# Two transformer blocks on one core: the RMS factor applied where results leave PSUM, squares folded in turn by VectorE, differential-output squares summed by ScalarE

## The reference, cut to what matters

```
xn = rms_norm(x, attn_norm[l])                      # x * rsqrt(mean(x*x)+eps) * gain
h  = xn @ w_in[l]                                   # [512, 2848], split in nine parts
c_q, c_kv = rms_norm(h_cq), rms_norm(h_ckv)         # "latent" parts, normed again
...
o_b = (softmax(q1 k1) - lam * softmax(q2 k2)) @ v   # 4 differential heads, each normed again
...
x = x + concat(o_a, o_b, o_c) @ w_o[l]
xn = rms_norm(x, ffn_norm[l])
g, u = split(xn @ w_gate_up[l])
x = x + (silu(g) * u) @ w_down[l]
```

## Time and profile before

| | us |
|---|---|
| median of 3 runs (3102.61 to 3106.01) | 3104.69 |
| the profiled execution | 3114.65 |
| its span | 3112.9 |
| its mean granted TensorE clock | 0.953 |

### The profile page before, as it was taken

The page is one execution under the profiler, slowest core; times in us unless marked ns, Lnnn a source line. Parts: engine busy times, 40 slices in busy tenths (PEclk is TensorE's granted clock), DMA queues, the critical chain, the costliest instruction groups (busy, mean ns, idle before and its releaser), DMA issues.

```text
span 3112.9 us, 33268 instructions
## 1 busy us (share of the span) xinstructions
PE 2881.9 (93%) x13076; PEld 2060.8 (66%) x13076; DVE 1189.6 (38%) x1632; ACT 949.3 (30%) x1558; POOL 810.6 (26%) x630
## 2 busy tenths in 40 slices
PE   5988989999899899899998999799998999899997
PEld 4965747888697575688885555445665444378886
DVE  2378614333318772443322233425323100243322
ACT  4448512222243862222221333323222100122222
POOL 5566502336637552133571000000000000000000
PEclk7999999999999999999998999898998999899998
DMA  4330013444422100334452110111112122133231
GB/s 101 86 86 17 1 39 104 142 138 145 137 75 70 39 1 22 104 115 142 137 161 87 41 41 27 28 27 41 41 41 54 54 64 71 41 95 95 86 93 65
DMA packets 382091, 230.25 MB, mean 74 GB/s; under 512 B 9228, under 2 KB 376716, under 8 KB 381936
## 3 DMA queue, kind: packets, MB, share of 16 engines
q1 hardware_dynamic: 379184, 223.04, 24.4%
q0 software_dynamic: 2224, 2.99, 0.8%
q10 hardware_dynamic: 528, 2.10, 0.2%
HBM read 226.01 MB, written 2.10 MB: 73 GB/s over the span
## 4 chain that ended last, share of the span: by engine, by line
PE 72%; DVE 13%; ACT 7%; DMA 6%; issue 2%; POOL 1%; SPq 0%; ACTq 0%; DVEq 0%; POOLq 0%
PE ps L728 61%; PE scores L728 8%; DMA raws<-in_w_down 4%; DVE R L1816 1%; PE ps L871 1%; ACT wH L1567 1%; DVE R L1926 1%; DVE R L520 1%; DVE R L521 1%; DVE R L511 1%; DVE R L512 1%; DVE R L515 1%; DVE xL L1922 0%; DVE x_lows L1922 0%; DVE wL L1948 0%
## 5 line engine op out<-in xcount | busy, mean ns | idle before, releaser
L728 PE MATMUL ps<-xH,wH 128*128 128x512 f32 x992 | 393.1, 396 | 12.0 <-DVE xL L1922 12.0
L728 PE MATMUL ps<-xH,wL 128*128 128x512 f32 x992 | 387.8, 391 | 0.0
L728 PE MATMUL ps<-xL,wH 128*128 128x512 f32 x992 | 387.7, 391 | 0.0
L638 POOL TENSOR_TENSOR U<-U 128x512 f32<-128x512 f32 x42 | 57.7, 1374 | 1193.2 <-ACT U L1390 1191.8
L1567 ACT ACTIVATE wH<-raws 128x2048 fp32r<-128x2048 f32 (+1 forms) x114 | 192.9, 1692 | 568.1 <-PE ps L728 393.6
L1948 DVE TENSOR_TENSOR wL<-raws,wH 128x2048 fp32r<-128x2048 f32 (+1 forms) x114 | 241.8, 2121 | 269.6 <-ACT wH L1567 262.7
L728 PE MATMUL ps<-R,ring 128*128 128x512 f32 x704 | 305.6, 593 | 2.9 <-DVE R L2166 1.6
L728 PE MATMUL ps<-U,ring 128*128 128x512 f32 (+4 forms) x640 | 270.5, 575 | 8.2 <-ACT R L1628 8.2
L728 PE MATMUL ps<-R 128*64 128x128 f32 (+3 forms) x1688 | 239.8, 332 | 37.5 <-DVE R L1835 10.2
L728 PEld LDWEIGHTS ps<-R 128*64 128x64 f32 (+2 forms) x1688 | 157.5, 165 | 135.1 <-issue 75.5
L728 PEld LDWEIGHTS ps<-R,ring 128*128 128x128 f32 x704 | 133.4, 190 | 170.7 <-issue 166.8
(11 more groups left out here) (344 smaller groups left out, 4275.5 us busy)
## 6 DMA issues: line engine op xcount, KB each, us to landing
raws<-in_w_gate_up SPq DMA_DIRECT2D x88, 512.0 KB, 5.2
ring<-in_w_in SPq DMA_DIRECT2D x34, 1024.0 KB, 6.4
spare<-in_w_ada SPq DMA_DIRECT2D x64, 512.0 KB, 4.0
raws<-in_w_down SPq DMA_DIRECT2D x32, 704.0 KB, 5.6
raws<-in_w_ffn_in SPq DMA_DIRECT2D x44, 512.0 KB, 4.7
ring<-in_w_in SPq DMA_DIRECT2D x32, 512.0 KB, 6.0
raws<-in_w_ffn_out SPq DMA_DIRECT2D x16, 704.0 KB, 4.3
ring<-in_w_o SPq DMA_DIRECT2D x5, 896.0 KB, 5.0
```

The costliest lines, as they stand in the source:

```text
L638: pg.do(nc.gpsimd.tensor_tensor(xn[:, 0, :], xn[:, 0, :], xn[:, k, :], ALU.add), folded if k == KT - 2 else None)
L728: return nc.tensor.matmul(o, a, b, start=first, stop=last)
```

## The change

1. **Factor after the product.** In the layers, VectorE writes x·gain only (`gained`), and ScalarE and VectorE split that. The factor goes in when results leave PSUM: by ScalarE's copy with a scale for the token-major pieces of W_IN (`scaled_out`), and in the FFN by VectorE, once on the gate before Silu and once on the product (`scaled_products`). The latent parts are left without it, since they are normed again; to be exact, eps over the squared factor is added to their sum of squares by one more product each (`square_sum`, operand `eps_`).
2. **Squares in turn.** ScalarE squares tile k as soon as it is there (`square_in_turn`), VectorE adds it up (`fold`) in place of GpSimd. TensorE takes the sums after the first gate group of an FFN (`stream_sums`), or after the first token group of layer 1. In layer 0 ScalarE squares the input in its own layout, four tiles of 128x1024, with the accumulator.
3. **Start.** The input comes in two halves behind the identity matrix, and the first W_IN piece's low part is VectorE's.
4. **Weights earlier.** The last W_O piece has a buffer of its own (`wo_last`), so that FFN weights are loaded and split before W_O ends; the first W_IN piece of layer 1 is loaded and split before the FFN of layer 0 ends. W_O is four pieces in both layers.
5. **Rotation.** It starts after the 16 differential sums, with a reciprocal of its own, and two of its steps go behind each of the 12 grouped-query sums.
6. **Differential-output squares.** ScalarE takes them with its accumulator, two of 128x128 in each of rounds 20 to 27; VectorE's four are gone.
7. **Tables.** A dummy Sqrt (`root_table`) sets ScalarE's table ahead of the root, at the start, at the W_O and FFN ends and before the second block's FFN. There GpSimd takes the low part of the first weight tile (`first_low`).

The diff, cut to its core:

```diff
-            return x_lows[:, k, :] if k < KT - 1 else x_low_last[:, :]
+            return UP[:, 2 * k:2 * k + 2, 0:256] if k < KT // 2 else xL1[:, k - KT // 2, :]
...
+        wo_last = R[:, 6656:6656 + 10 * 256].rearrange("p (k c) -> p k c", k=10)
...
+        DB_RING = [D_BANKS[1], D_BANKS[0]]
+        NB = SP[1][:, 0, :]
...
-        WO = [[(0, 384), (384, 768), (768, 1024)], [(0, 256), (256, 512), (512, 768), (768, 1024)]]
+        WO = [(0, 256), (256, 512), (512, 768), (768, 1024)]
...
-        OUTPUT_SQUARES_AT, OUTPUT_ROOT_AT = (21, 22, 23, 24), 26
+        OUTPUT_SQUARES_FROM, OUTPUT_ROOT_AT = 20, 27
...
+            def first_low(l):
+
+                g = l * NF
+                pool.wait_ge(wh_ready, g + 1)
+                pg.do(nc.gpsimd.tensor_tensor(wL[:, g % 2, :], raws[:, g % 2, :], wH[:, g % 2, :].bitcast(F32), ALU.subtract),
+                      first_wl_ready)
...
-                    q = a - l * N_ADA + ADA_FIRST
-                    if q >= FT + 4 and (q - FT) % 2 == 0:
-                        fold((q - FT) // 2 - 2)
-                fold(KT - 2)
-                pg.seen[sq_ready] += 1
+                if l + 1 < L:
+                    low_part(l + 1, 0)
...
+            def two_sums(bank, total, last):
+
+                for n, square in enumerate((total, last)):
                     if n == 0:
-                        pp.more(folded)
+                        pp.more(folded, KT - 2)
...
+            def stream_sums(l):
+
+                if l > 0:
+                    pe.wait_ge(inv_copied, l)
+                two_sums(NB, PTb[:, 0, :], PTb[:, 1, :]).then_inc(sums_full, 1)
...
-            def square_sum(k0, k1, src, ready):
+            def square_sum(k0, k1, src, ready, eps_):
                 bank = ab.fill(pe)
+                pp.more(lat_eps_ready)
+                mm(bank[:, :], ones[:, :], eps_, True, False)
                 for k in range(k0, k1):
                     pp.more(ready)
-                    ins = mm(bank[:, :], ones[:, :], src(k), k == k0, k == k1 - 1)
+                    ins = mm(bank[:, :], ones[:, :], src(k), False, k == k1 - 1)
...
+                            if l > 0 and a == c1 and t == 0:
+                                stream_sums(l)
...
-                folded_sums()
-                spread_roots(S)
+                if l < L:
+                    pe.wait_ge(a_free, ab.n)
+                else:
+                    folded_sums(X(0), X(KT - 1))
+                    spread_roots(S)
...
+                            if l < L and q == 0:
+                                if n == 0:
+                                    stream_sums(l)
+                                else:
+                                    pp.more(diag_ready)
+                                    mm(NB[:, :], ones[:, :], dg[:, :], True, True).then_inc(spread_full, 1)
...
-            sp.dma_start(xin, A["x"][0].rearrange("(t p) c -> p t c", p=P)).then_inc(x_in, 16)
-            sp.dma_start(ident[:, :], A["c_ident"][:, :]).then_inc(x_in, 16)
...
+            sp.dma_start(ident[:, :], A["c_ident"][:, :]).then_inc(x_in[0], 16)
+            for a in range(2):
+                half = slice(a * D // 2, (a + 1) * D // 2)
+                sp.dma_start(xin[:, :, half], A["x"][0].rearrange("(t p) c -> p t c", p=P)[:, :, half]).then_inc(x_in[a], 16)
...
-                for piece in layer_pieces(l):
-                    load(piece)
+                for j, piece in enumerate(layer_pieces(l)):
+                    if l > 0 and j == 0:
+                        sp.wait_ge(wl_ready, l * NF - 1)
+                    if l > 0 and j == 1:
+                        sp.wait_ge(*f_by[l * NF - 1])
+                    load(j, piece)
+                sp.wait_ge(ot_full, (l + 1) * (N_PAIR - N_DIFF) // TT)
+                for dst, src in wo_piece(l, *WO[-1])(None):
+                    sp.dma_start(dst, src).then_inc(wo_in, 16)
...
+            def square_in_turn(k):
+                ap.more(x_ready)
+                if k >= 2:
+                    act.wait_ge(folded, turns * (KT - 2) + k - 1)
+                ap.do(f(PTb[:, min(k, 1), :], xT[:, k, :], ACT.Square), sq_ready)
+
+            def root_table():
+                ap.do(f(unused[:, :], eps[:, :], ACT.Sqrt))
+
...
+            for t in range(TT):
+                ap.do(f(xin[:, t, :], xin[:, t, :], ACT.Square, accum_out=ssg[:, t:t + 1]))
+            ap.do(f(rt[:, :], ssg[:, :], ACT.Sqrt, bias=eps[:, :], scale=1.0 / D), root_ready)
...
+            def scaled_out(dst, src, t, sem=None):
+                ap.do(f(dst, src, ACT.Copy, scale=rt[:, t:t + 1]), sem)
...
+                    if 0 <= p_ - OUTPUT_SQUARES_FROM < 2 * TT:
+                        for n in range(2):
+                            t, h = divmod(2 * (p_ - OUTPUT_SQUARES_FROM) + n, BH)
+                            ap.do(f(vtmp[:, 0, 0:BV], O[:, t, h * BV:(h + 1) * BV], ACT.Square, accum_out=ssO[:, t, h:h + 1]))
...
+                root_table()
+                for k in range(KT):
+                    high_tile(xH[:, k, :], k)
+                    square_in_turn(k)
+                    if k >= 5 and k < 7:
+                        split_high(l, k - 5)
+                stream_root()
+                turns += 1
...
+                        if l < L:
+                            act.wait_ge(gate_scaled, n)
+                            ap.do(f(Pb[:, q % 2, :], Pb[:, q % 2, :], ACT.Silu), silu_ready)
...
-                def output_squares(t):
-                    if t == 0:
-                        dve.wait_ge(v_done, (l + 1) * N_DIFF)
-                    o = O[:, t, :]
-                    vp.do(v.tensor_tensor(vtmp[:, 0, 0:512], o, o, ALU.mult))
-                    vp.do(v.tensor_reduce(ssO[:, t, :], vtmp[:, 0, 0:512].rearrange("p (h d) -> p h d", h=BH), AX.X, ALU.add))
...
+                turning = chain(*[rotation(vp, v, t, T, rs, vtmp, 16, BD, gB, ropeB, bT_ready, l, 8, False) for t in range(TT)])
                 for c in range(GK):
                     for t in range(TT):
                         sums(ssG[:, t, c:GH:GK], (3, GD))
+                        next(turning)
+                        next(turning)
...
+                    gained(m, first_gain(l, KT))
+                    low_part_of(xH[:, m, :], xl(m), m)
+                    if m == 6:
+                        split_low(l, 0)
+                    fold(m)
+                split_low(l, 1)
+                vp.more(root_ready)
+                vp.do(v.reciprocal(rt[:, :], rt[:, :]))
+                vp.do(v.tensor_tensor(dg[:, :].rearrange("p (a b) -> p a b", a=TT), bc(ident[:, :], TT, 1),
+                                      bc(rt[:, :], P, 2), ALU.mult), diag_ready)
+                dve.wait_ge(spread_full, l + 1)
+                vp.do(v.tensor_copy(inv, NB[:, :]), inv_copied)
...
+            def gained(k, gain):
+                vp.do(v.tensor_scalar(Pb[:, k % 2, :], xT[:, k, :], gain(k), None, ALU.mult), scaled)
+
+            def fold(k):
+                nonlocal squares
+                squares += 1
+                if 1 <= k < KT - 1:
+                    dve.wait_ge(sq_ready, squares)
...
+            def scaled_products(l):
+                for j in range(FT):
+                    n = l * FT + j + 1
+                    dve.wait_ge(gate_full, n)
+                    vp.do(v.tensor_tensor(Pb[:, j % 2, :], A_BANKS[j % 2][:, :], inv, ALU.mult), gate_scaled)
+                    bank = db.take(dve)
+                    vp.more(silu_ready)
+                    t = PTb[:, 1, :]
+                    vp.do(v.tensor_tensor(t, Pb[:, j % 2, :], bank[:, :], ALU.mult), d_free)
+                    vp.also(silu_used)
+                    split_low(l, j + 2)
+                    vp.do(v.tensor_tensor(t, t, inv, ALU.mult))
+                    split(hH[:, j, :], hL[:, j, :], t, h_ready)
```

381 lines of the change are left out of this document (243 added, 138 removed).

## The result

| | before | with the change |
|---|---|---|
| median, us | 3104.72 (4 runs) | 3034.01 (4 runs, 3030.29 to 3040.21) |
| profiled execution, us | 3114.65 | 3035.83 |
| its span | 3112.9 | 3034.0 |
| its mean granted clock | 0.953 | 0.970 |

The ratio is 0.9775, with a 95% interval of 0.9757 to 0.9793: 70.7 us less by the medians. 94.3 less was forecast. The kernel is faster, as forecast, but by a quarter less: 3034.01 for 3010.4, a hundredth of a microsecond above the upper end of the range (3034). One run of the kernel before, among those taken beside the experiments, took 8896.47 us; it is left out of the ratios, and its cause is not known.

What follows compares the result with a forecast made beforehand. TensorE was taken as the bound, fully busy inside FFN tiles, with only its idle time between them to save. The terms summed to 94.3 us less, from a median of 3104.69 to 3010.4; range 2998 to 3034.

Steps and rivals of the forecast that it cites:

- Bound: FFN tiles: TensorE busy 238.00 of 238.00 us at full clock; only its idle time between such stretches can go.
- Entries: From W_O through tile 0 of both layers' FFNs: 13.6 us in place of 28.65, 29.8 saved for the two.
- The start: Program start: first W_IN piece done at 39.5 us, where it ended at 62.83; 23 saved, bounds 18 to 25.
- layer 1's second token group: Entry of layer 1: from last residual addition to this group's copy 8.3 us, for 26.8; 18.5 saved.
- The step that failed: W_O and down tiles: the fold's eight VectorE additions of 0.69 us lie beside them, with no cost counted.
- Rotation: Both layers: TensorE's 12.3 us of waiting go, plus 3 for the lower clock behind; 15.5 saved, bounds 12.3 to 16.6.
- Added: TensorE: four more products of the eps diagonals cost 4.0 us.
- Attention: Attention rounds: VectorE's squares moved to ScalarE save 3.7 us a layer, 7.4 in all, bounds -3 to 11.
- Second FFN: Second block's FFN entry: split leaves VectorE and table load comes ahead, 2.8 us saved; 0.9 if GpSimd blocks VectorE.
- VectorE in the FFN: 44 gate/up tiles: VectorE's two more operations of 0.69 us a tile cost 0, covered by its idle time.
- Rival B: W_IN pieces: GpSimd's low part blocks VectorE, TensorE waits at most 15 us in two layers; 3025, chance 0.15.
- Rival E: FFN gate path: Silu and VectorE's in-order list lengthen the 44 gate/up tiles, making the kernel slower; 3115, chance 0.03.

Runs made afterwards that it cites:

- run 10: The changed kernel with the loads of each layer's FFN weights held until W_O has ended: 3062.96 us, ratio 0.9845.
- run 1: The changed kernel with SyncE issuing the next FFN weight tile's load ahead of the conditioning load: 3013.93 us, ratio 0.9701.
- run 8: The changed kernel with the rotation steps behind all grouped-query sums again, its own early reciprocal kept: 3038.03 us, ratio 0.9760.
- run 7: The changed kernel with two more unused VectorE products of 128x512 in each of the 44 gate/up tiles: 3039.93 us, ratio 0.9777.
- run 5: The changed kernel with the second block's weight pieces starting at ring slot 2: 3034.44 us, ratio 0.9770; with its first FFN low part on VectorE too, 3031.87, 0.9755.
- run 6: The changed kernel with GpSimd's 22 small head-gain loads issued before its first low part, not between its low parts: 3045.94 us, ratio 0.9805.

## Why the forecast fell short

- **Bound.** Right for the gate/up tiles, which stayed at full rate, as in the earlier trace rows; wrong for the down tiles, for which no row was read.
- **Entries.** Right in mechanism. The FFN's gave 15.7 each for 14.9 (by the prediction's own 28.65 - 13.6 it is 15.05 each, 30.1 for the two and not 29.8); 11 of it hang on the weights and 4 to 5 on the rest (run 10). The start gave 24.4 at the end of the first piece for 23, less some 5 for the new stall; layer 1's second token group came 9.2 us behind the addition for 8.3.
- **The step that failed:** the term that puts everything laid beside the down tiles at nothing ("the fold's eight additions of 0.69 lie beside W_O and the down tiles", and ScalarE's new x tiles there with no word at all). Cover was read as idle time of the engine, and ScalarE was indeed idle, 6.7 us ahead of a high part. But its list is part of a loop through SyncE, whose turn was 8.1 us against tiles of 7.72 and which lived on a lead of 8 us. The turn became 8.98 in layer 0, by the x tiles (0.30) and the later landing of the loads (0.60), and 8.54 in layer 1, by the landing alone, and the lead was used up at down tile 4. That was 22.9 us; with one load moved in SyncE's list the same work costs nothing (run 1). VectorE's additions are not in the loop. No row said that the landing would be longer, and why it is stays open.
- **The rest of the sum.** With the 22.9 it would have been 71.4, against 70.7 by the medians. That this is so near is partly luck: single terms missed by up to 4 us, and both ways.
- **Rotation.** The wait went, as the term said (12.3 and the clock), but not for the reason given: without the interleaving only 0.83 us of waiting is left in each layer (run 8). Its size is right by luck.
- **Added.** The four eps products took 0.86 each, 3.4 for 4.0.
- **Attention.** 5.4 for 7.4 (1.4 and 4.0). The squares' rounds gain what was read, and a part is given back around the root.
- **Second FFN.** A loss of 0.3 to 1.2 for a gain of 2.8. The lock was priced (0.9), the slot of the ring was not looked at; with the slot right 1.1 to 1.2 are gained, near the table load alone.
- **VectorE in the FFN.** Zero, right (run 7). Rival B did not show: no wait on a W_IN low part stands in TensorE's list beyond the first piece. Rival E's mechanism was in the wrong place: the gate/up tiles had room, the down tiles had none.

## What to carry to other kernels

Idle time of an engine is cover only if the engine is not a link in a loop through other queues. Take one turn of each such loop (issue, landing, each operation behind it in its list, the wait that lets the next issue go), compare it with the tile, and look at how the lead changes from tile to tile: a lead that shrinks says that the loop is slower than it looks. And where a counter of buffers is started anew, see which piece comes to lie in the slot that somebody waits for.

## What the runs showed of the hardware

- A VectorE operation of 0.49 took 4.68 us beside a GpSimd operation of 4.50 and ended 0.3 behind it (after the change, 2633.72); one with a PSUM operand beside such a GpSimd operation kept its 0.75 (run 5, 2630.66).
- With 22 loads of 32 to 64 KB around them, the ring's pieces of 1 MB took twice as long to land: 12.0 us with them and 5.1 without for the fourth piece, 27.4 and 13.9 for the first three (run 6 and the change).
- The same 1344 products of the second block and what lies between them took 1022.2 to 1023.3 us in eleven executions (mean granted clock 0.961 to 0.963) and 1031.8 to 1032.0 in three (0.951), whatever the edit. Two profiled executions have to be aligned product by product before their difference is read.
- The FFN weights' loads landed later in every kernel with the change (second block's down weights: 4.6 or 4.7 us for 4.3 and 4.4). The cause is open.
